# Expert layer: gate groups applied two steps later, gates read back in four parts, searches and row fetches spread differently

## The chip, the cores and the metric

The kernel runs on one core of one Trainium2 chip. The metric is the time of one execution on the device in microseconds (us). Before the change three executions took 3490.39, 3495.34 and 3495.37 us, median 3495.34. The profiled execution is a fourth one.

## The reference, cut to what matters

The reference is a stack of two transformer blocks followed by a third block (512 tokens, width 1024, all fp32). The change touches only the end of it, a layer of retrieved experts:

```
def peer_layer(h, w_q, sub_keys, u_tab, v_tab):          # T = 512 tokens, 8 heads, 128 x 128 experts
    q = (hf @ w_q).reshape(T, 8, 2, 128)
    s = einsum('thpd,hpnd->thpn', q, sub_keys)           # 128 scores for each half key
    sc, idx = top_k(s, 16)                               # for each half
    cand = sc[:, :, 0, :, None] + sc[:, :, 1, None, :]   # 256 sums
    top_sc, pos = top_k(cand, 16)                        # 16 experts per head, 128 per token
    eidx = take_along_axis(cidx, pos)
    gate = softmax(top_sc)
    act = gelu(einsum('thkd,td->thk', u_tab[eidx], hf))
    y   = einsum('thk,thkd->td', gate * act, v_tab[eidx])
```

Before that stand, in this order: two blocks with gated delta-net or stick-breaking attention, memory attention and an MLP, and one block with HGRN2, convolution and output projection.

## The kernel before, in words

The first 2130 us or so (all layers up to the experts) are not touched. The expert layer treats its four blocks of 128 tokens in two ways.

*By rows* (blocks 0 and 1). For each token, its 128 chosen expert rows are fetched from the table `peer_uv` (down and up vector side by side, 8 KB for each of 128 tokens). There are NROW = 256 such rows. Each row r costs one indirect DMA on GpSimd (L1287, waiting for `row_added` of the row that held its place before), one dot product on VectorE (`dot_row`, L3572), two tiny operations on ScalarE (`weigh_row`, L2699 and L2701: gelu and gate), and one multiply-add on VectorE (`add_row`, L3584). Ten places hold rows in flight; five of them, and in the gate stage only these, are outside the weight array.

*Densely* (blocks 2 and 3, 256 tokens). All 16384 experts are computed in 128 pairs of items. An "up" item (`up_unit`, L2025) multiplies 128 experts' down vectors with all 256 tokens, ScalarE takes the gelu into `weights` (L2668); a "down" item (`down_unit`, L2040) adds those weights times the up vectors into four banks that stay open. Each item loads 512 KB through the SP queue (L1088) into one of RAWS = 4 buffers; the load of item n waits for the end of item n - 4. Between the up and down items each weight has to be multiplied by the token's gate, which is zero for unchosen experts. The gates of 8 tokens (one group, NGATE = 32 groups) are made by 8 matmuls of one-hot matrices (`gate_products`, L2053): VectorE writes the one-hots (`one_hots`, L3534 and L3537), GpSimd two of them (`second_ones`, L1301), ScalarE scales six of them by the gate (`scale_ones`, L2689). The first half of the gates is applied at once on VectorE (`gate_weights`, L3548); ScalarE copies the second half out of the banks (`keep_gates`, L2677) and stores it in DRAM (`gate_half`, L2681). Two pairs of banks (4/5 and 6/7) alternate between groups.

The order of all engines follows one list, `STEPS`: 64 up items (the first stage; up to step 34 the query projection runs beside them), 32 gate groups (the gate stage), 128 alternating down and up items (the mixed stage, from `MIX_AT`), 4 "back" steps, then 64 down items (the last stage). Each engine walks the list in its own loop. The 256 rows are spread over it by `row_step`: 64 in the first stage, 10 in the gate stage, 120 in the mixed stage, 2 in the back steps, 60 in the last stage. The searches for the top 16 (`search`, a generator cut into pieces, eight for two heads) are handed out by `search_steps`: those of blocks 0, 2 and 3 in the first stage, those of block 1 (four groups, 32 pieces) one piece in each of 32 steps from `MIX_AT + 2` on.

The second half of the gates comes back from DRAM by `load_gates` on the SP queue (L1099), between item loads, and is applied by `later_weights` (L3560): in BACKS = 2 parts of 32 groups each, 128 KB a load, into LOADS = 8 buffers. Part 0 is applied one group a step from `MIX_AT + 67` on; part 1 in the four back steps, when all up items are done. The first down item of the second half (L2037) waits until every part is applied.

The names in the listing: `rows_at[s]` are the rows of step s, `gathers_at[s]` the fetches issued there, `full(engine, t)` waits until a bank is written, `have` until it is read out.

## Time and profile before

| | us |
|---|---|
| median of three executions | 3495.34 |
| profiled execution, its own time | 3504.54 |
| its span | 3502.8 |
| first stage and gate stage, from 2133 to 2718 | 585 |
| mixed stage, from 2718 to 3222 | 504 |
| back steps, from 3222 to 3247 | 25 |
| last stage and end, from 3247 | 256 |

The profiled execution took 9.2 us longer than the median. Over its whole span TensorE was busy for 92%, VectorE for 63%, ScalarE for 28%, GpSimd for 51%. In the two slices of the page that hold the gate stage the granted clock of TensorE is 6 tenths, elsewhere 9 or more. The bounds of the stages are read from the first and last matmuls of each line; busy times of a window are given as time and, in brackets, number of instructions.

### The profile page before, as it was taken

The numbers are of one execution on the slowest core, as the hardware profiler recorded it, in microseconds if no ns is written. First come the engines' busy times: TensorE is split into PE (matmuls) and PEld (weight loads), VectorE is DVE, ScalarE is ACT, GpSimd is POOL, SyncE is SP. The second block draws the span as 40 slices with busy tenths as digits, with TensorE's granted clock in tenths as the row PEclk, the third lists the DMA queues.
The fourth block names the chain that finished last, engine by engine and source line by source line (L and its number), as shares of the span: only waits on it lengthen the run. The fifth ranks groups of instructions, "written<-read, shape, count | busy, mean of one in ns | idle before, by whom it ended". The sixth has DMA issues, their size and how long they took to land.

```text
span 3502.8 us, 38167 instructions
## 1 busy us (share of the span) xinstructions
PE 3229.5 (92%) x13780; PEld 2400.8 (69%) x13780; DVE 2197.4 (63%) x3621; ACT 964.7 (28%) x2176; POOL 1797.9 (51%) x1008
## 2 busy tenths in 40 slices
PE   8999899999999999999999999997855989887998
PEld 5769778886767888688776677866755655554433
DVE  5764453337674333579465875889855996666765
ACT  4564431112174111211133423222344221111111
POOL 3544269997203999788865571222343343333420
PEclk9999999999999999999999999999966999999999
DMA  4430022232301322223322126767823899999996
GB/s 163 166 132 1 25 85 96 96 108 96 132 37 50 107 96 96 96 87 136 118 80 95 37 100 227 301 243 274 293 104 117 341 364 417 405 406 369 395 417 272
DMA packets 122368, 628.66 MB, mean 179 GB/s; under 512 B 13400, under 2 KB 21720, under 8 KB 66648
## 3 DMA queue, kind: packets, MB, share of 16 engines
q1 hardware_dynamic: 77104, 343.07, 26.6%
q0 software_dynamic: 36864, 268.45, 19.6%
q10 hardware_dynamic: 8232, 14.95, 1.1%
q8 instruction: 99, 1.62, 0.2%
q14 instruction: 69, 0.57, 0.1%
HBM read 607.55 MB, written 18.87 MB: 179 GB/s over the span
## 4 chain that ended last, share of the span: by engine, by line
PE 66%; DVE 15%; DMA 10%; ACT 4%; issue 4%; POOL 2%; DVEq 0%; ACTq 0%; POOLq 0%; SPq 0%
PE bank L1455 13%; PE bank L1456 13%; PE bank L1457 13%; PE bank L2040 6%; PE bank L2025 5%; DMA residual<-in_peer_vd 5%; DMA residual<-in_peer_ut 3%; DVE arena L3572 2%; ACT branch L2689 1%; DVE weight_ring L3584 1%; DVE squares L3403 1%; PE bank L1901 1%; PE bank L1883 1%; PE bank L1769 1%; PE bank L1402 1%
## 5 line engine op out<-in xcount | busy, mean ns | idle before, releaser
L1457 PE MATMUL bank<-split_arena 128*128 128x512 f32 x1776 | 696.8, 392 | 0.0
L1287 POOL DMA_INDIRECT arena<-in_peer_uv,rstd x181 | 266.4, 1472 | 633.0 <-DVE weight_ring L3584 345.7
L1194 POOL TENSOR_TENSOR split_arena<-weight_ring,ones 128x1024 fp32r<-128x1024 f32 x204 | 505.8, 2480 | 153.2 <-PE bank L1457 101.0
L1455 PE MATMUL bank<-split_arena 128*128 128x512 f32 x1392 | 546.7, 393 | 5.2 <-DVE split_normed L2930 2.5
L1456 PE MATMUL bank<-split_arena 128*128 128x512 f32 x1392 | 542.0, 389 | 0.0
L2025 PE MATMUL bank<-normed,residual 128*128 128x256 f32 x2048 | 481.4, 391 | 50.9 <-ACT arena L2668 38.6
L1196 POOL TENSOR_TENSOR split_arena<-weight_ring,split_arena 128x1024 fp32r<-128x1024 f32 x204 | 518.5, 2542 | 16.0
L2040 PE MATMUL bank<-residual,arena 128*128 128x512 f32 x1024 | 475.5, 611 | 45.4 <-DVE arena L3560 24.6
L2025 PEld LDWEIGHTS bank<-normed,residual 128*128 128x128 f32 x2048 | 396.6, 196 | 153.8 <-issue 65.6
L2040 PEld LDWEIGHTS bank<-residual,arena 128*128 128x128 f32 x1024 | 193.8, 194 | 288.4 <-issue 226.6
L1457 PEld LDWEIGHTS bank<-split_arena 128*128 128x128 f32 x1776 | 334.7, 188 | 73.5
L1163 POOL TENSOR_TENSOR split_arena<-weight_ring,split_arena 128x1024 fp32r<-128x1024 f32 x54 | 129.4, 2405 | 402.6 <-ACT split_arena L2179 350.7
L1455 PEld LDWEIGHTS bank<-split_arena 128*128 128x128 f32 x1392 | 261.6, 188 | 67.9 <-issue 8.6
L1456 PEld LDWEIGHTS bank<-split_arena 128*128 128x128 f32 x1392 | 261.6, 188 | 54.6 <-issue 1.5
L2699 ACT ACTIVATE row_gelu<-dots 128x1 f32<-128x1 f32 x256 | 51.6, 202 | 690.1 <-DVE dots L3572 689.9
L3572 DVE CUSTOM_DVE_ANT_0 arena<-arena,branch 128x1024 f32<-128x1024 f32 x181 | 220.3, 1221 | 34.0 <-DMA arena<-in_peer_uv,rstd 33.8
L1455 PE MATMUL bank<-split_normed,split_arena 128*128 128x512 f32 x560 | 223.7, 399 | 4.8 <-DVE split_arena L3207 3.8
L1456 PE MATMUL bank<-split_normed,split_arena 128*128 128x512 f32 x560 | 222.6, 397 | 0.0
L1287 POOL DMA_INDIRECT weight_ring<-in_peer_uv,rstd x75 | 106.0, 1414 | 190.1 <-DVE branch L3584 102.5
L2220 ACT ACTIVATE squares<-squares 128x512 f32<-128x512 f32 x64 | 40.4, 632 | 486.6 <-DVE squares L2845 486.6
L3220 DVE SCALAR_TENSOR_TENSOR bank<-arena,vector_columns,bank 128x512 f32<-128x512 f32 x232 | 153.3, 753 | 0.1
L2845 DVE SCALAR_TENSOR_TENSOR squares<-bank,rstd 128x512 f32<-128x512 f32 x64 | 44.1, 692 | 170.4 <-PE bank L1457 154.2
(509 smaller groups left out, 5265.6 us busy)
## 6 DMA issues: line engine op xcount, KB each, us to landing
residual<-in_peer_ut SPq DMA_DIRECT2D x128, 512.0 KB, 7.2
residual<-in_peer_vd SPq DMA_DIRECT2D x128, 512.0 KB, 11.1
weight_ring<-in_w_up SPq DMA_DIRECT2D x32, 1024.0 KB, 4.8
weight_ring<-in_w_down SPq DMA_DIRECT2D x32, 1024.0 KB, 4.7
weight_ring<-in_w_in SPq DMA_DIRECT2D x32, 1024.0 KB, 4.8
weight_ring<-in_ada_w SPq DMA_DIRECT2D x24, 1024.0 KB, 4.8
weight_ring<-in_w_in_a SPq DMA_DIRECT2D x12, 1024.0 KB, 6.7
weight_ring<-in_w_out SPq DMA_DIRECT2D x12, 1024.0 KB, 6.9
```

What stands on the lines that cost most here:

```text
L1163: pool.tensor_tensor(lo, raw(u)[:, :, h * P:(h + 1) * P], f32(hi), ALU.subtract).then_inc(split_ready, 1)
L1194: pool.tensor_tensor(hi, part, bc_mid(ones[:], DT), ALU.mult).then_inc(split_hi, 1)
L1196: pool.tensor_tensor(lo, part, f32(hi), ALU.subtract).then_inc(split_ready, 1)
L1287: pool.indirect_dma_start(row_places[i][0], None, a["peer_uv"], bass.IndirectOffsetOnAxis(ap=experts[n][:, c:c + 1], axis=0)).then_inc(row ...
L1455: pe.matmul(psum[t.bank][:], hi, a_hi[k], start=first, stop=False)
L1456: pe.matmul(psum[t.bank][:], lo, a_hi[k], start=False, stop=False)
L1457: return pe.matmul(psum[t.bank][:], hi, a_lo[k], start=False, stop=last)
L2025: m = pe.matmul(psum[t.bank][:, 0:DENSE], blk(raws[n % RAWS], k), H[:, k, DENSE:], start=k == 0, stop=k == DT - 1)
L2040: x = pe.matmul(psum[2 * b + c][:], blk(weights[:, m % WHALF, :], b), raws[n % RAWS][:, 512 * c:512 * (c + 1)], start=m == 0, stop=m == NK ...
L2699: act.activation(w, dots[:, r % RING8:r % RING8 + 1], ACT.Gelu).then_inc(row_gelu, 1)
L3220: m = dve.scalar_tensor_tensor(acc[i] if j < CONV_B - 1 else Y[:, k + i, :], glu[:, k + i, j:j + SEQ], vcol("conv_w_2", j * DT + k + i), a ...
L3572: dve.tensor_tensor_reduce(row, row, h_tok[:, n, :], 1.0, 0.0, ALU.mult, ALU.add, dots[:, r % RING8:r % RING8 + 1]).then_inc(row_dot, 1)
```

## The change

Four edits.

- In a gate step q, VectorE now writes the one-hots of group q and then applies the gates of group q - 2 (before: q - 1). ScalarE copies out group q - 2 ahead of scaling the one-hots of group q (before: group q - 1 behind it). Groups 30 and 31 are both finished in the first mixed step. The banks and buffers are the same.
- The 32 search pieces of block 1 stand in every fourth mixed step over 128 steps instead of in every one of the first 32.
- The second half of the gates comes back in BACKS = 4 parts of 16 experts' columns: 128 loads of 64 KB instead of 64 of 128 KB, into LOADS = 16 buffers of half the size (the same memory). Parts 0, 1 and 2 are applied in the mixed stage, two groups a step for 16 steps each, part 3 in the back steps, of which there are now two. The loads are placed by `back_load`: the first 16 of a part in pairs from 4 items ahead of the part's end, the other 16 in pairs 12 items behind it; for part 3 the latter all at item 195.
- 50 rows in the first stage instead of 64, and 24 in the gate stage instead of 10.

```diff
-LOADS = 8
-BACKS = 2
+LOADS = 16
+BACKS = 4
@@ in the plan
-        BACK_ITEM = WHALF + WHALF + 4
-        back_at = {MIX_AT + WHALF + 3 + q: q for q in range(NGATE)}
+        back_at = {MIX_AT + 2 * BACK_J * (p + 1) + 3 + i: (p, 2 * i) for p in range(BACKS - 1) for i in range(NGATE // 2)}
+        back_load = {}
+        for p in range(BACKS):
+            base = WHALF + 2 * BACK_J * (p + 1)
+            for i in range(NGATE):
+                n = base - 4 + i // 2 if i < LOADS else base + 12 + (i - LOADS) // 2
+                back_load.setdefault(min(n, 3 * WHALF + RAWS - 1), []).append(NGATE * p + i)
...
-        search_steps += range(MIX_AT + 2, MIX_AT + 2 + 64)
+        search_steps += range(MIX_AT + 2, MIX_AT + 2 + 32 * 4, 4)
...
-        gate_back = [k[:, i * UNIT_N:(i + 1) * UNIT_N] for k in keys_t for i in range(4)]
+        gate_back = [blk(k, i) for k in keys_t for i in range(8)]
...
-        for a0, a1, rows in ((3, G_AT, 64), (G_AT, MIX_AT, 10), (MIX_AT, BACK_AT, 120), (BACK_AT, LAST_AT, 2), (LAST_AT, LAST_AT + 58, 60)):
+        for a0, a1, rows in ((3, G_AT, 50), (G_AT, MIX_AT, 24), (MIX_AT, BACK_AT, 120), (BACK_AT, LAST_AT, 2), (LAST_AT, LAST_AT + 58, 60)):
@@ SyncE
-                elif BACK_ITEM <= n < BACK_ITEM + NGATE + LOADS:
-                    load_gates(n - BACK_ITEM)
-                elif n == 3 * WHALF + RAWS - 1:
-                    for q in range(NGATE + LOADS, BACKS * NGATE):
-                        load_gates(q)
+                for i in back_load.get(n, ()):
+                    load_gates(i)
+                if n == 3 * WHALF + RAWS - 1:
                     sp.dma_start(H[:, :, :], x_dram).then_inc(x_back, 16)
@@ ScalarE
+                if s < MIX_AT + 1 and s >= 2 and STEPS[s - 2][0] == "gate":
+                    keep_gates(STEPS[s - 2][1])
+                if s == MIX_AT:
+                    keep_gates(NGATE - 1)
                 if kind == "gate":
                     scale_ones(v)
-                if s and STEPS[s - 1][0] == "gate":
-                    keep_gates(STEPS[s - 1][1])
@@ VectorE
                 if kind == "gate":
                     one_hots(v)
-                    if v:
-                        gate_weights(v - 1)
+                    if v >= 2:
+                        gate_weights(v - 2)
                 elif kind == "back":
                     for q in range(LOADS * v, LOADS * (v + 1)):
-                        later_weights(1, q)
+                        later_weights(BACKS - 1, q)
                 elif s == MIX_AT:
+                    gate_weights(NGATE - 2)
                     gate_weights(NGATE - 1)
...
                 if s in back_at:
-                    later_weights(0, back_at[s])
+                    p, q = back_at[s]
+                    later_weights(p, q)
+                    later_weights(p, q + 1)
```

The order of VectorE in the middle of the gate stage, before. `mem_keys` and `mem_values` are the two one-hot buffers (even and odd groups), banks 4 and 5 hold even groups, 6 and 7 odd ones; `ISA` is a row's dot product, `SCALAR_TENSOR_TENSOR` a row's multiply-add:

```order
L3534 TENSOR_TENSOR mem_keys<-arena,masks 128x1024
L3537 TENSOR_TENSOR branch<-arena,masks 128x768
L3548 TENSOR_TENSOR arena<-arena,bank6 128x64x4
L3548 TENSOR_TENSOR arena<-arena,bank7 128x64x4
L3572 ISA weight_ring,dots<-weight_ring,branch 128x1024
L3572 ISA dots 128x1
L3534 TENSOR_TENSOR mem_values<-arena,masks 128x1024
L3537 TENSOR_TENSOR branch<-arena,masks 128x768
L3548 TENSOR_TENSOR arena<-arena,bank4 128x64x4
L3548 TENSOR_TENSOR arena<-arena,bank5 128x64x4
L3584 SCALAR_TENSOR_TENSOR weight_ring<-weight_ring,row_gelu 128x1024
```

And the same place now (the lines of the changed file are 5 higher here):

```order
L3539 TENSOR_TENSOR mem_keys<-arena,masks 128x1024
L3542 TENSOR_TENSOR branch<-arena,masks 128x768
L3553 TENSOR_TENSOR arena<-arena,bank4 128x64x4
L3553 TENSOR_TENSOR arena<-arena,bank5 128x64x4
L3577 ISA weight_ring,dots<-weight_ring,branch 128x1024
L3577 ISA dots 128x1
L3539 TENSOR_TENSOR mem_values<-arena,masks 128x1024
L3542 TENSOR_TENSOR branch<-arena,masks 128x768
L3553 TENSOR_TENSOR arena<-arena,bank6 128x64x4
L3553 TENSOR_TENSOR arena<-arena,bank7 128x64x4
L3589 SCALAR_TENSOR_TENSOR weight_ring<-weight_ring,row_gelu 128x1024
L3577 ISA arena,dots<-arena,branch 128x1024
```

Behind the one-hots of an even group now stand the products of the even group before it, not those of the odd group just computed, and rows follow more often.

SyncE's queue around the back steps, before; the waits are on `item_done` (`expert_unit_done`) and on `gate_used`:

```order
L1088 DMA residual<-in_peer_vd 128x1024 [waits expert_unit_done] x4
L1099 DMA mem_keys<-gate_half 128x256 [waits gate_half_used] x4
L1099 DMA mem_values<-gate_half 128x256 [waits gate_half_used] x4
L1099 DMA mem_keys<-gate_half 128x256 [waits gate_half_used] x4
L1099 DMA mem_values<-gate_half 128x256 [waits gate_half_used] x4
L1099 DMA mem_keys<-gate_half 128x256 [waits gate_half_used] x4
L1099 DMA mem_values<-gate_half 128x256 [waits gate_half_used] x4
L1116 DMA normed<-residual_copy 128x4096
```

And now:

```order
L1093 DMA residual<-in_peer_vd 128x1024 [waits expert_unit_done]
L1104 DMA mem_values<-gate_half 128x128 [waits gate_half_used] x2
L1093 DMA residual<-in_peer_vd 128x1024 [waits expert_unit_done]
L1104 DMA mem_values<-gate_half 128x128 [waits gate_half_used] x2
L1093 DMA residual<-in_peer_vd 128x1024 [waits expert_unit_done]
L1104 DMA mem_values<-gate_half 128x128 [waits gate_half_used] x2
L1104 DMA mem_keys<-gate_half 128x128 [waits gate_half_used] x8
L1104 DMA mem_values<-gate_half 128x128 [waits gate_half_used] x8
L1119 DMA normed<-residual_copy 128x4096
```

Behind the last item load of the mixed stage stood 24 loads of 128 KB; now 18 of 64 KB, and 14 more of the last part stand in pairs ahead of it, between the item loads.

## Rows read from the trace of the kernel before

**Rows 1.** Windows: PE, PEld, DVE, ACT, POOL busy us; granted clock, DMA share, GB/s.
```profile
2133.00:2320.00 187.00, 181.04 (x856) 144.51 (x855) 155.48 (x449) 54.12 (x134) 46.88 (x35) 0.99 0.76 282
2320.00:2523.00 203.00, 174.29 (x756) 142.23 (x754) 187.06 (x549) 57.81 (x150) 52.62 (x36) 0.94 0.78 283
2523.00:2718.00 195.00, 105.80 (x512) 98.66 (x512) 111.75 (x159) 81.97 (x277) 82.58 (x76) 0.67 0.31 111
2718.00:2850.00 132.00, 125.62 (x415) 81.16 (x416) 124.56 (x334) 27.86 (x85) 47.59 (x29) 0.96 0.93 358
2850.00:2990.00 140.00, 130.79 (x428) 81.31 (x427) 95.78 (x131) 26.11 (x91) 48.94 (x36) 0.98 1.00 402
2990.00:3222.00 232.00, 212.55 (x697) 133.53 (x695) 143.13 (x195) 36.24 (x139) 89.33 (x56) 0.96 1.00 402
3222.00:3247.00 25.00, 0.42 (x2) 0.42 (x2) 15.20 (x38) 1.38 (x5) 2.23 (x1) 0.60 0.84 300
```

**Rows 2.** Waits in the gate stage, 2523 to 2720: us, times, longest.
```profile
DVE arena L3548 <- ACT weight_ring L2677: 82.9, 32, 5.6
```

**Rows 3.** Timeline of two gate groups: start, duration, engine, operation, idle before.
```profile
2577.34 1.22 DVE L3534 TENSOR_TENSOR mem_values<-arena,masks 128x1024 f32<-128x1024 f32 x1
2579.47 1.86 ACT L2689 ACTIVATE branch<-branch,masks 128x128 f32<-128x128 f32 x6 [2.82 <-DVE branch L3537]
2581.54 3.75 PE L2053 MATMUL bank<-branch,mem_values 128*128 128x128 f32 x16 [1.47 <-issue]
2581.89 0.75 DVE L3548 TENSOR_TENSOR arena<-arena,bank 128x256 f32<-128x256 f32 x2 [2.46 <-ACT weight_ring L2677]
2582.56 1.22 DVE L3572 CUSTOM_DVE_ANT_0 arena<-arena,branch 128x1024 f32<-128x1024 f32 x1
2583.71 1.22 DVE L3534 TENSOR_TENSOR mem_keys<-arena,masks 128x1024 f32<-128x1024 f32 x1
2588.93 1.28 DVE L3584 SCALAR_TENSOR_TENSOR weight_ring<-arena,row_gelu,weight_ring 128x1024 f32<-128x1024 f32 x1
2590.13 1.22 DVE L3534 TENSOR_TENSOR mem_values<-arena,masks 128x1024 f32<-128x1024 f32 x1
```

**Rows 4.** GpSimd's one-hots (ns min/median/max; timeline, same columns) and a fetch.
```profile
L1301 POOL TENSOR_SCALAR branch<-arena,masks x64: 780/791/3661, 2523.4 to 2706.3; 128x128 f32<-128x128 f32 x64
...
2565.67 3.41 POOL L1301 TENSOR_SCALAR branch<-arena,masks 128x128 f32<-128x128 f32 x2 [2.10 <-PE bank L2053]
2572.48 1.75 POOL L1287 DMA_INDIRECT arena<-in_peer_uv,rstd  x1 [3.41 <-DVE weight_ring L3584]
```

**Rows 5.** Waits at the end of the first stage, 2330 to 2523.
```profile
PE bank L2025 <- ACT arena L2668: 25.8, 11, 4.4
```

**Rows 6.** VectorE's row adds, 2720 to 2850, grouped by line: busy us, mean ns.
```profile
L3584 DVE SCALAR_TENSOR_TENSOR weight_ring<-arena,row_gelu,weight_ring 128x1024 f32<-128x1024 f32 x19 | 24.4, 1283 | 4.0 <-ACT row_gelu L2701 3.5
L3584 DVE SCALAR_TENSOR_TENSOR weight_ring<-weight_ring,row_gelu 128x1024 f32<-128x1024 f32 x10 | 12.8, 1281 | 1.8 <-ACT row_gelu L2701 1.7
```

**Rows 7.** DMA queue 1 (packets, MB, share) and gate loads in two windows, 3250 to 3440 and 2990 to 3210.
```profile
q1 hardware_dynamic: 6935, 25.25, 33.5%
...
q1 hardware_dynamic: 13112, 33.45, 39.4%
...
mem_values<-gate_half SPq DMA_DIRECT2D x19, 128.0 KB, 12.0
mem_keys<-gate_half SPq DMA_DIRECT2D x16, 128.0 KB, 11.3
```

**Rows 8.** Waits for the gate loads in the mixed stage, 2980 to 3230.
```profile
DVE arena L3560 <- DMA mem_keys<-gate_half: 27.1, 9, 7.1
```

**Rows 9.** Timeline of the back steps.
```profile
3223.05 1.98 SPq L1099 DMA_DIRECT2D mem_keys<-gate_half  x4
3231.38 1.43 DVE L3560 TENSOR_TENSOR arena<-arena,mem_keys 128x256 f32<-128x256 f32 x4 [4.86 <-DMA mem_keys<-gate_half]
3246.61 9.75 PE L2040 MATMUL bank<-residual,arena 128*128 128x512 f32 x17 [24.58 <-DVE arena L3560]
```

More of the change, by code:

```diff
@@ L620, in build, with blk @@
         v_tiles = [item_tile(2 * NKEY - 1, b) for b in range(4)]
+        def blk(ap, n):
+            return ap[:, n * P:(n + 1) * P]
         q_f = region(0, LH)
@@ L977, in f32 @@
             return ap.bitcast(F32)
-        def blk(ap, n):
-            return ap[:, n * P:(n + 1) * P]
         def raw(u):
```

## The prediction

> **What bounds the kernel now.** I read the windows by stage first [rows 1], since the page's shares average over stages with different limits. Five limits follow one another there.
>
> From 2133 to 2320 TensorE is busy 181.0 of 187 us. From 2320 to 2523 it is busy 174.3 of 203, VectorE 187.1: there VectorE sets the pace, for up items wait for a bank that ScalarE empties late (25.8 us, [rows 5]), and ScalarE works in order behind the weighing of rows, which waits for VectorE's dot products. In the gate stage (195 us) nothing is full: TensorE 105.8, VectorE 111.8, ScalarE 82.0, DMA share 0.31, clock 0.67. That is a chain. In the first mixed window both TensorE (125.6 of 132) and VectorE (124.6) are nearly full and the DMA share is 0.93; from 2850 to 3222 the DMA share is 1.00 at 402 GB/s. In the back steps TensorE stands for 24.6 us behind `later_weights` [rows 9].
>
> The chain of the gate stage is seen in two groups of the timeline [rows 3]. VectorE starts one-hots at 2577.34, ScalarE scales from 2579.47 for 1.86 us and only then copies out the group before, VectorE multiplies that from 2581.89, after an idle 2.46 us, and at 2582.56 it is free again: 5.22 us a group, of which VectorE works 2.08 + 0.67. The waits add up to 82.9 us in 32 groups [rows 2]. A row adds its two big operations: the dot product 1.15 (2582.56 to 2583.71) and the add 1.20 (2588.93 to 2590.13), together 2.35. 32 x 5.22 + 10 x 2.35 = 190.5 us, and with the first group's start that is the 195 measured.
>
> **Gate stage, -41.** Now ScalarE copies group q - 2 ahead of the scaling, when its matmuls are long done, so the 82.9 us of waits go. What is late next? Two loops. VectorE's own work is 2.08 + 0.67 a group and 2.35 for each of 24 rows: 32 x 2.75 + 24 x 2.35 = 144.4 us, 4.5 a group. The other loop goes over two groups, since banks and one-hot buffers alternate: one-hots 2.08, scaling 1.86, matmuls 3.75 at 1.2 GHz [rows 3], and some 0.3 for four hand-overs: 8.0 for two groups, 4.0 a group or 128 us. VectorE's is the longer one. Two groups with two rows take VectorE 10.2 us, two with one row 7.85, so the second loop shows only in the latter, and hardly. With 6 us to start (the first matmuls come 6 us behind the window's beginning, since one-hots, scaling and one-hots on GpSimd stand in line) and 4 to finish groups 30 and 31 in one step, I take 154 us instead of 195: -41. The bounds: with VectorE busy all the time, -48 (147: the 111.8 busy us of [rows 1] plus 14 rows of 1.22 + 1.28 [rows 3]); with a step that stays at 5.22 for groups and hides the rows only in part, -15 (a rival, below). If TensorE's clock went to 2.4 GHz here the matmuls would halve, but VectorE would still pace. The waits added (none is new: the same semaphores one group earlier) hold nobody: behind VectorE's wait stand rows, and it has none to make.
>
> **First stage, -14.** 14 rows fewer are 14 x 2.35 = 33 us less for VectorE. By the planner's weights (32 steps of 6.1, 29 of 3.6) 9 of them leave the part beside the query projection, where TensorE is at 181.0 of 187: that gives 1 or 2 us at most. Five, and one or two of the 9 that fall behind 2320, leave the part that VectorE paces: 6.5 x 2.35 = 15 us. There VectorE would need 172, TensorE 174.3 of 203 before; two engines that are nearly equal don't overlap fully, so I take 190 for this window, -13, and -1 for the other. Bounds: -8 (half of it is waiting of another sort) and -28 (all of TensorE's idle time there).
>
> **Mixed stage, -6 and +10.** The block-1 searches: in the 130 us from 2720 VectorE adds 19 + 10 rows [rows 6], 29 x 2.35 = 68 us, of 124.6 busy, so searches are about 55. Three quarters of it, 41 us, move behind 2850, where VectorE is busy 239 of 372 us [rows 1]: it fits, VectorE goes to about 75%. In the first window TensorE then needs no waits, but the bytes are there too: 358 GB/s for 132 us is what 402 GB/s moves in 118. Between 0 and -14 I take -6, nearer to the middle, since TensorE was busy 125.6 already.
>
> The gate reload: the same 8.4 MB in twice as many packets. The price of a packet from [rows 7]: in the last stage queue 1 takes 33.5% of 16 x 190 us for 25.25 MB of 4 KB packets, 40.3 us of engine time per MB, 165 ns a packet. From 2990 to 3210 it takes 39.4% of 16 x 220 = 1387 us for 33.45 MB; 19 + 16 = 35 gate loads of 128 packets of 1 KB are 4.59 MB, the other 28.86 MB cost 1163 at 40.3, so 4480 small packets cost 224 us, 50 ns each. A straight line through 1 KB: 50 and 4 KB: 165 gives 31 ns for 512 B. Before, the mixed stage had 40 loads: 5120 x 50 / 16 = 16 us of all 16 engines. Now it has 110 (three parts of 32 and 14 of the last): 14080 x 31 / 16 = 27. The DMA share is 1.00 there, so the 11 us count nearly in full: +10. Bounds: +4 (a packet costs by its bytes alone, 25 ns) and +28 (50 ns whatever its size). That VectorE multiplies 96 halves with more instructions costs it some 5 us, hidden in its idle time, and 64 more issues cost SyncE 64 x 0.5 us [rows 9], hidden too: it waits for items nearly all the time.
>
> The Trainium skill says in "DMA: Bandwidth & Descriptors", section Bandwidth, that transfers under 64 KB are descriptor-dominated and gives 0.95 us for one of 64 KB against 6.15 for 1 MB. By that, 110 loads would hold the engines for 104 us, not 27, and the change would lose more than it gains. The trace speaks against it: 35 loads of 128 KB between 2990 and 3210 went through while the share stayed at 1.00 and the rate at 402 GB/s, because transfers of both queues run side by side. It strengthens the slower rival.
>
> **Back steps, -9.** Now 24 loads stand behind the last item, in rounds of 8 buffers, and the landings are 8.3 us (3223.05 to 3231.38) for the first, so three rounds make 24.6 us [rows 9]. Afterwards 14 of 32 loads have landed; 18 remain, at 0.5 us an issue (1.98 for four) 9 us, then one landing of 3 to 8 us and a last multiplication: 9 + 5 + 1.5 = 15.5. That is -9; bounds -16 (issue alone decides) and -3 (8.3 for a landing, and a second round for buffers 14 and 15).
>
> **Sum.** -41 - 14 - 6 + 10 - 9 = -60. Against the profiled execution's own 3504.5 that is 3444.5; this execution was 9.2 us above the median of 3495.3, so I expect the median at 3435.3, say 3435.
>
> **The rivals.**
> *A. GpSimd paces the gate stage.* Its two one-hots wait for the matmuls of q - 2 and stand behind fetches, which wait for a row add. With more rows they run against VectorE's big operations more often. For it: the pair took 3.41 us once, and single ones between 780 and 3661 ns [rows 4]. Then two groups take a fetch or two of 1.75, 3.41 and 3.75 of matmuls: up to 10.7, 5.3 a group, 171 us with start and end 180: only -15 in the stage, total -34, 3461. Against: the median is 791, and a fetch is issued right behind the add, a step before the one-hots can start. "GPSIMD Engine Reference" of the Trainium skill, Key points, has it that GpSimd shares its SBUF interfaces with VectorE and contends with VectorE operations that read two SBUF inputs; the spread in [rows 4] agrees, the median doesn't.
> *B. The reload eats more.* 50 ns for 512 B: +28 instead of +10, total -42, 3453.
> *C. All slack is given back.* First stage -28, first mixed window -14, back -16, gate -48, reload +4: -102, 3393; with half of the excess 3414.
> *D. The gate stage doesn't change.* If the wait had another cause than the copy (the clock, or GpSimd), the chain stays at 5.22 and 14 more rows cost 33 us there, while the first stage gives 14: with the other terms 0 to +14, about no change, 3495 to 3510.
> *E. Slower: the reload stalls VectorE.* The second 16 loads of a part are issued three steps ahead of their use, as before, and now there are two a step in 24 more steps. A wait was 3.0 us in the mean (27.1 in 9) and 7.1 at most [rows 8]. VectorE has 372 - 239 = 133 us idle in the DMA-bound windows; searches and extra instructions take 46 of them, 87 remain. Over 48 steps with reloads (three parts, 16 steps each), it saturates from 1.8 us a step, and each us more costs 48; beyond 3.1 the change loses its 60. At 4 us a step in all 48: 48 x 4 - 87 = +105, less 60: 3540. Against: half of the loads now have 11 steps' notice, so 24 steps at 3.0 are 72, which still fits.
>
> **How the numbers follow.** Chances: forecast 0.58 (its own range 3417 to 3452), A 0.14, B 0.09, C 0.11, D 0.04, E 0.04. From A at 3461 with some margin to the middle of C: 3404 to 3468. Within 0.2% (7 us, about what this kernel's measurement can tell) of 3495 lies most of D: 0.03. Slower: E and the rest of D, 0.04. Faster: 0.93.
>
> **What would show it.** In the gate stage, VectorE's wait for the copy near 0, its busy share over 90%, the window near 154 us; 170 or more with TensorE waiting for GpSimd's one-hots is A. The window from the first up item to the gate stage 14 us shorter. In the mixed stage the time from first to last item about 4 us longer than 504, with share 1.00, and packets of 512 B at 31 ns (50 is B); VectorE's waits for loads under 80 us (else E). TensorE's idle time in the back steps near 15. The forecast is wrong above all if VectorE isn't what ends last in the gate stage.

## The result, and the profile after

The changed kernel takes 3445.35 us (median of four, 3436.92 to 3446.74) against 3492.86 before (3488.27 to 3495.37): a ratio of 0.986, interval 0.984 to 0.9881. The forecast was 3435, range 3404 to 3468. The profiled execution's span fell from 3502.8 to 3444.1, by 58.7 us, where the sum said 60. The terms did much worse than the sum: two errors of 19 and 16 us, of opposite sign, nearly cancelled. The stages are read from the first and last matmuls of three lines: L2028 up items, L2056 gate groups, L2043 down items. For the changed kernel (instructions and their ns min/median/max, first and last start):

```profile
L2028 PE MATMUL bank<-normed,residual x2048: 379/379/796, 2150.1 to 3168.9; 128*128 128x256 f32 x187
L2056 PE MATMUL bank<-branch,mem_keys x256: 274/418/553, 2501.2 to 2660.8; 128*128 128x128 f32 x128
L2043 PE MATMUL bank<-residual,arena x1024: 592/592/1219, 2667.8 to 3430.2; 128*128 128x512 f32 x171
```

So the first stage is 2150.1 to 2501.2, the gate stage 2501.2 to 2667.7, the mixed stage up to 3168.9. The same lines of before give 2148.6, 2529.3, 2718.2 and 3221.7. Side by side, in us:

| | before | changed | difference | forecast |
|---|---|---|---|---|
| first stage | 380.7 | 351.1 | -29.6 | -14 |
| gate stage | 188.9 | 166.5 | -22.4 | -41 |
| mixed stage | 503.5 | 501.2 | -2.3 | +4 |
| TensorE idle in the back steps | 24.6 | 15.4 | -9.2 | -9 |
| last stage and end | 256.5 | 259.8 | +3.3 | 0 |

(1.5 us more lie ahead of the first item.) The windows of the changed kernel, with the columns of [rows 1]:

```profile
2135.00:2320.00 185.00, 182.49 (x867) 146.14 (x866) 150.00 (x471) 54.52 (x129) 42.92 (x30) 0.99 0.72 264
2320.00:2495.00 175.00, 166.21 (x750) 138.83 (x748) 158.90 (x488) 53.87 (x127) 34.97 (x26) 0.96 0.76 271
2495.00:2668.00 173.00, 97.31 (x513) 91.17 (x514) 144.42 (x201) 89.97 (x305) 163.28 (x90) 0.72 0.57 194
2668.00:2800.00 132.00, 123.76 (x405) 78.32 (x405) 91.66 (x162) 23.52 (x83) 51.75 (x31) 0.96 0.99 397
2800.00:2940.00 140.00, 126.56 (x418) 81.83 (x418) 103.77 (x207) 24.54 (x87) 53.29 (x33) 0.96 0.99 392
2940.00:3169.00 229.00, 210.54 (x715) 137.72 (x713) 174.40 (x350) 40.33 (x144) 90.12 (x56) 0.98 1.01 401
```

Against [rows 1]: in the gate stage (third line) GpSimd, 82.6 of 195 us before, is now busy 163.3 of 173, while VectorE, which was to pace it, has 28 us to spare. In the first mixed window VectorE fell from 124.6 to 91.7 us, and the DMA share rose from 0.93 to 0.99. Who waited in the gate stage:

```profile
PE bank L2056 <- POOL branch L1304: 64.5, 18, 6.9
ACT weight_ring L2680 <- PE bank L2056: 21.1, 12, 4.0
DVE arena L3553 <- ACT weight_ring L2680: 4.5, 2, 3.9
```

The wait of [rows 2], 82.9 us in 32, is down to 4.5 in 2. TensorE waits 64.5 us for GpSimd's one-hots (L1304). That wait alone proves little, for it was there before too. These two rows are of the kernel before, 2523 to 2720:

```profile
PE bank L2053 <- POOL branch L1301: 73.9, 22, 6.9
POOL branch L1301 <- PE bank L2053: 70.0, 20, 4.4
```

Then GpSimd in its turn waited 70.0 us for TensorE, and its one-hots were 3% of the chain that ended last. Now it waits 1.8 us for TensorE. The price of its one-hots is in the row by line (busy us, mean ns of one):

```profile
L1304 POOL TENSOR_SCALAR branch<-arena,masks 128x128 f32<-128x128 f32 x64 | 118.7, 1864 | 13.7 <-ACT masks L2155 10.9 <-PE bank L2056 1.8
```

and the chain that ended last through this stretch, by line, is clear:

```profile
by line: POOL branch L1304 67.9%; POOL arena L1290 13.7%; POOL weight_ring L1290 10.4%; PE bank L2056 4.5%; issue 3.9%; ACT weight_ring L2680 0.4%; PE bank L2043 0.4%; DVE arena L3553 0.3%; DVEq L3588 0.0%; POOLq L1283 0.0%; ACTq L935 0.0%
```

Before, the same 64 instructions took 63.0 us, 991 ns each; 92% of the chain is now GpSimd's one-hots and fetches. The timeline shows when they are slow:

```profile
2583.93 1.57 POOL L1304 TENSOR_SCALAR branch<-arena,masks 128x128 f32<-128x128 f32 x2
2585.60 1.22 DVE L3539 TENSOR_TENSOR mem_values<-arena,masks 128x1024 f32<-128x1024 f32 x1 [2.60 <-PE bank L2056]
...
2587.77 8.56 POOL L1304 TENSOR_SCALAR branch<-arena,masks 128x128 f32<-128x128 f32 x4
2588.27 1.28 DVE L3589 SCALAR_TENSOR_TENSOR weight_ring<-weight_ring,row_gelu 128x1024 f32<-128x1024 f32 x1
2589.47 1.22 DVE L3577 CUSTOM_DVE_ANT_0 arena<-arena,branch 128x1024 f32<-128x1024 f32 x1
2590.61 1.22 DVE L3539 TENSOR_TENSOR mem_keys<-arena,masks 128x1024 f32<-128x1024 f32 x1
2591.75 1.04 DVE L3542 TENSOR_TENSOR branch<-arena,masks 128x768 f32<-128x768 f32 x1
2592.44 3.75 PE L2056 MATMUL bank<-branch,mem_values 128*128 128x128 f32 x16 [3.96 <-POOL branch L1304]
```

Two one-hots take 1.57 us while VectorE stands idle (2583.93), and four take 8.56 beside its uninterrupted operations (from 2587.77), 2.1 each. TensorE starts on a group when that group's two are done, at 2592.44 for the first pair. Laid beside VectorE's operations in the two traces, 51 of the 64 one-hots before overlap none of them (by less than 0.05 us) and take 790 ns in the mean; in the changed kernel only 12 do, with 794 ns. An estimate from the same overlaps: the 64 one-hots are 50.6 us of work at 790 ns. In the changed kernel 5.0 us of their time lay beside no operation of VectorE, 21.7 beside `gate_weights` (one input in PSUM) and 92.6 beside operations whose large inputs both lie in SBUF. If they ran at full speed in the first two, the other 23.9 us of work took 92.6 us: about a quarter of the speed.

In the back steps the loads of part 3 follow one another now:

```profile
3171.10 1.71 DVE L3565 TENSOR_TENSOR arena<-arena,mem_keys 128x128 f32<-128x128 f32 x8 [5.85 <-ACT arena L2671]
3172.49 4.29 SPq L1104 DMA_DIRECT2D mem_keys<-gate_half  x8
3174.96 0.49 DVE L3565 TENSOR_TENSOR arena<-arena,mem_values 128x128 f32<-128x128 f32 x2 [2.16 <-DMA mem_values<-gate_half]
3176.83 4.03 SPq L1104 DMA_DIRECT2D mem_values<-gate_half  x8
3182.77 1.70 DVE L3565 TENSOR_TENSOR arena<-arena,mem_values 128x128 f32<-128x128 f32 x8
3184.61 2.04 PE L2043 MATMUL bank<-residual,arena 128*128 128x512 f32 x2 [15.36 <-DVE arena L3565]
```

With [rows 9] this is 15.36 us of idle TensorE against 24.58. The 16 last loads are issued at 0.5 us each, from 3172.49 to 3180.86, but VectorE waits for none of them. It waits, last at 3179.60, for the loads issued just ahead; the chain has one landing of 8.03 us there, from 3171.54:

```profile
3171.54 8.03 DMA mem_values<-gate_half
```

Behind it come VectorE's own 4.9 us: two groups, a row's dot product and the last 16 groups.

### The profile page after: what moved, and what is told of

It reads as the page before. It is cut to its first block, busy times and chain, and to the rows that moved or that the text cites. A ratio compares the mean times of both kernels' runs of the same rounds, so it can differ in the third digit from the quotient of the medians.

```text
span 3444.1 us, 38297 instructions
## 1 busy us (share of the span) xinstructions
PE 3208.0 (93%) x13780; PEld 2395.6 (70%) x13780; DVE 2201.9 (64%) x3685; ACT 968.3 (28%) x2176; POOL 1869.0 (54%) x1008
## 4 chain that ended last, share of the span: by engine, by line
PE 74%; DMA 9%; DVE 7%; POOL 6%; ACT 2%; issue 2%; SPq 0%; DVEq 0%; ACTq 0%; POOLq 0%
PE bank L1458 13%; PE bank L1459 13%; PE bank L1460 13%; PE bank L2028 10%; PE bank L2043 8%; DMA residual<-in_peer_vd 6%; POOL branch L1304 3%; DMA residual<-in_peer_ut 2%; PE bank L1975 2%; PE bank L1904 1%; PE bank L1886 1%; PE bank L1772 1%; PE bank L1405 1%; PE bank L1650 1%; PE bank L1660 1%
## 5 line engine op out<-in xcount | busy, mean ns | idle before, releaser
L2028 PE MATMUL bank<-normed,residual 128*128 128x256 f32 x2048 | 479.1, 390 | 42.6 <-DMA residual<-in_peer_ut 34.3
L2028 PEld LDWEIGHTS bank<-normed,residual 128*128 128x128 f32 x2048 | 398.4, 196 | 138.2 <-DMA residual<-in_peer_ut 48.3
L2043 PE MATMUL bank<-residual,arena 128*128 128x512 f32 x1024 | 467.1, 603 | 28.2 <-DVE arena L3565 15.4
L2043 PEld LDWEIGHTS bank<-residual,arena 128*128 128x128 f32 x1024 | 192.1, 192 | 263.2 <-issue 213.9
L3577 DVE CUSTOM_DVE_ANT_0 arena<-arena,branch 128x1024 f32<-128x1024 f32 x178 | 216.9, 1219 | 18.8 <-DMA arena<-in_peer_uv,rstd 18.7
L1290 POOL DMA_INDIRECT weight_ring<-in_peer_uv,rstd x78 | 120.9, 1550 | 184.4 <-DVE branch L3589 99.0
L3589 DVE SCALAR_TENSOR_TENSOR weight_ring<-arena,row_gelu,weight_ring 128x1024 f32<-128x1024 f32 x92 | 117.8, 1281 | 62.7 <-ACT row_gelu L2704 60.5
```

The costliest lines, as they stand in the source:

```text
L1290: pool.indirect_dma_start(row_places[i][0], None, a["peer_uv"], bass.IndirectOffsetOnAxis(ap=experts[n][:, c:c + 1], axis=0)).then_inc(row ...
L2028: m = pe.matmul(psum[t.bank][:, 0:DENSE], blk(raws[n % RAWS], k), H[:, k, DENSE:], start=k == 0, stop=k == DT - 1)
L2043: x = pe.matmul(psum[2 * b + c][:], blk(weights[:, m % WHALF, :], b), raws[n % RAWS][:, 512 * c:512 * (c + 1)], start=m == 0, stop=m == NK ...
L3577: dve.tensor_tensor_reduce(row, row, h_tok[:, n, :], 1.0, 0.0, ALU.mult, ALU.add, dots[:, r % RING8:r % RING8 + 1]).then_inc(row_dot, 1)
L3589: m = dve.scalar_tensor_tensor(row_acc[n], row, w, row_acc[n], ALU.mult, ALU.add)
```

## The experiments

My theory after the traces: the gate stage is paced by GpSimd (rival A of the prediction); every row taken from the first stage is worth most of its 2.35 us; of the two edits in the mixed stage one gains and the other loses it. Twelve runs. "Before" below is the kernel before in the same series (medians 3496.10, 3498.08 and 3497.19 in the three series). The changed kernel was timed only with the result, where before had 3492.86, so a difference from it in us compares two series whose level differs by 3 to 5 us. The profiled execution of before, 3504.54, lies 6 to 12 us above all these medians.

**a_two_behind.** The first edit alone.

```diff
@@ ScalarE: keep_gates of group q - 2, ahead of scale_ones(q); VectorE:
-                    if v:
-                        gate_weights(v - 1)
+                    if v >= 2:
+                        gate_weights(v - 2)
```

> The kernel before with only the first edit: gates applied and copied out two groups later, rows (64 and 10), searches and the two-part reload as before. From first matmul of the gate stage to the first down item it took 188.9 us before and 166.5 with all edits. Theory 1 (GpSimd's one-hots, slowed by VectorE, pace the gate stage once the copy is off the chain): with 14 fewer rows there are fewer fetches and fewer big VectorE operations beside them, so about 145 us, the one-hot pairs on GpSimd still above 2 us in the mean, and the total 40 to 45 us below before. Theory 2 (the loop of VectorE's one-hots, scaling and matmuls at 1.2 GHz paces): 4.0 us a group, 128 to 135 us, total 53 to 60 below. First stage unchanged at 381 (within 3) by both.

Measured: 3455.10 us, ratio 0.988 (0.9865 to 0.9894), -41 us. Gate stage 143.2 (theory 1 had said 145), first stage 378.8. GpSimd's one-hots took 1868 ns each in the mean. They are 58.6% of the chain through the stage, in which VectorE is busy only 75% of the time. So GpSimd is in the way even with 10 rows, and the edit alone gives most of the change's gain.

**b_rows.** The fourth edit alone.

```diff
-        for a0, a1, rows in ((3, G_AT, 64), (G_AT, MIX_AT, 10), ...
+        for a0, a1, rows in ((3, G_AT, 50), (G_AT, MIX_AT, 24), ...
```

> The kernel before with only the row edit: 50 rows in the first stage, 24 in the gate stage. First stage (first up item to first gate matmul, 380.7 before, 351.1 with all edits): by the prediction's term 14 us shorter, by the trace of the changed kernel 30 shorter, which I now expect, since no other edit touches that stage. Gate stage with the old order: each row adds its 2.35 us to a chain of 5.22, so 188.9 + 33 = 222. If instead rows fall into the 2.46 us waits, under 200. Total with the chain: about +3 (between -2 and +8); with rows in the waits: -20.

Measured: 3505.05, ratio 1.0019 (1.001 to 1.0028), +9. First stage 350.4, as in the changed kernel; gate stage 219.7. In the old chain a row costs 2.2 us (30.8 for 14), nearly its full 2.35, so alone the edit gives back in the gate stage what it wins in the first. Beside the first edit it pays a little: against a_two_behind the changed kernel's first stage is 27.7 us shorter and its gate stage 23.3 longer.

**c_search.** The second edit alone.

```diff
-        search_steps += range(MIX_AT + 2, MIX_AT + 2 + 64)
+        search_steps += range(MIX_AT + 2, MIX_AT + 2 + 32 * 4, 4)
```

> The kernel before with only the search edit: block 1's 32 search pieces in every fourth mixed step. The prediction took -6 for it. If the early mixed window was held by VectorE: mixed stage (first down item to last up item, 503.5 before) about 6 shorter, total -6 (to -12). If DMA bytes hold the whole mixed stage, what is won early is lost later: within 3 us of no change.

Measured: 3482.98, ratio 0.996 (0.9946 to 0.9974), -13. The mixed stage is 484.7, not 503.5: three times the forecast's term. (With the stage's code unchanged, a_two_behind and b_rows have 501.1 and 501.4, so 16 to 19 us are won there; the timed runs show 13 in all.) The whole mixed stage, before and in this run:

```profile
2718.00:3222.00 504.00, 468.96 (x1536) 296.01 (x1536) 363.47 (x657) 90.21 (x315) 185.86 (x120) 0.97 0.98 390
```

```profile
2713.00:3197.00 484.00, 459.86 (x1534) 290.24 (x1533) 361.09 (x653) 88.35 (x314) 196.95 (x120) 0.99 1.00 403
```

The same work at 403 instead of 390 GB/s, and TensorE's idle time 24 us instead of 35, its busy time 9 shorter at a mean clock of 0.99 instead of 0.97.

**d_back.** The third edit alone (BACKS = 4, LOADS = 16 and the placing of loads and products).

```diff
-LOADS = 8
-BACKS = 2
+LOADS = 16
+BACKS = 4
```

> The kernel before with only the reload in four parts. The prediction took +10 in the mixed stage for smaller packets and -9 in the back steps, together about 0. The trace of the changed kernel has 15.4 us of idle TensorE in the back steps instead of 24.6, and a mixed stage of 501.2 instead of 503.5 with searches spread as well. If small packets cost by bytes plus a few ns (27 ns seen): mixed stage +3 to +6, total -4 to -6. If the +10 is there and the search edit hid it: total 0.

Measured: 3507.47, ratio 1.0027 (1.0016 to 1.0037), +11: neither expectation. Mixed stage 514.8 (+11.3, where the prediction had +10), idle TensorE in the back steps 10.9 (-13.6), last stage and end 260.6 instead of 256.5. By its trace the edit comes out even, by its timed runs it loses; the trace of before is of an execution 8.4 us above this series' median, that of d_back 2 below its own, and this is most of the difference. Against the 501.1 and 501.4 of a_two_behind and b_rows the mixed stage is over 13 us longer. Like the row edit it is no gain alone; two_parts below asks whether it is one in company.

**hot1 and hot0.** Less of the one-hot work on GpSimd, from the changed kernel.

```diff
-POOL_HOT = 2
+POOL_HOT = 1
```

> The changed kernel with one second-side one-hot a group on GpSimd instead of two (VectorE and ScalarE take seven instead of six). VectorE gets 0.14 us a group more, ScalarE 0.31. If GpSimd paces the gate stage (its pair took 1.6 us alone and 4.3 to 5.5 beside VectorE's operations): gate stage 166.5 to about 152, total 12 to 15 below the changed kernel. If VectorE paces: gate stage about 4 us longer. If the matmuls at 1.2 GHz pace: unchanged.

```diff
-POOL_HOT = 2
+POOL_HOT = 0
@@ TensorE
-                pe.wait_ge(pool_hot, q + 1)
@@ GpSimd
-                    second_ones(v)
+                    pass
```

> The changed kernel with all eight second-side one-hots on VectorE and ScalarE, none on GpSimd (and TensorE doesn't wait for GpSimd in the gate stage). VectorE has 2.08 + 0.27 + 0.67 = 3.02 us a group and 24 x 2.35 for rows: 153 us, so a gate stage of about 157: 9 us below the changed kernel if GpSimd paces it now, and 9 us above it if VectorE does.

Measured: 3434.47 (ratio 0.9819, 0.98 to 0.9838) and 3436.85 (0.9821, 0.9804 to 0.9838). Gate stages 150.5 and 151.3 instead of 166.5, nearly the length of VectorE's own work. The window and the chain of hot1 in that stage:

```profile
2499.00:2650.00 151.00, 93.82 (x513) 87.10 (x514) 144.23 (x197) 95.20 (x328) 117.47 (x57) 0.73 0.69 229
```

```profile
by line: PE bank L2056 32.0%; issue 11.2%; DVE branch L3542 9.5%; ACT branch L2692 8.8%; DVE weight_ring L3589 8.8%; DVE mem_values L3539 7.3%; DVE mem_keys L3539 6.6%; DVE arena L3553 5.9%; DVE arena L3577 4.5%; DVE weight_ring L3577 3.8%;
```

No GpSimd line is left in the chain; VectorE is busy 144.2 of 151. The stage is close to what the prediction's sum for VectorE gave (144.4 plus ends), and the GpSimd term is 16 of the 19 us that were missing. In the total 8.5 to 11 us of them arrive by the medians, 14 by the ratios to before: the mixed stage was 513 and 514, 501 in the changed kernel (below).

**rows57 and rows43.** The row edit in other sizes, from the changed kernel.

```diff
-        for a0, a1, rows in ((3, G_AT, 50), (G_AT, MIX_AT, 24), ...
+        for a0, a1, rows in ((3, G_AT, 57), (G_AT, MIX_AT, 17), ...
```

> The changed kernel with 57 rows in the first stage and 17 in the gate stage. By the traces 14 rows gave 29.6 us in the first stage, 2.1 us a row: first stage 366. Gate stage: with GpSimd pacing, each row costs a fetch of 1.5 to 2 us and the contention of two big operations, so 7 fewer give about -14, 152; with VectorE pacing 7 x 2.35 = -16. Total within 3 us of the changed kernel.

```diff
-        for a0, a1, rows in ((3, G_AT, 50), (G_AT, MIX_AT, 24), ...
+        for a0, a1, rows in ((3, G_AT, 43), (G_AT, MIX_AT, 31), ...
```

> The changed kernel with 43 rows in the first stage and 31 in the gate stage. TensorE is busy 348.7 of the 360 us before the gate stage now, so the first stage can give only 5 to 8 us more, while the gate stage grows by 15 (7 x 2.1 to 2.35): total +8. If the first stage still gave 2.1 us a row: total 0.

Measured: 3447.73 (0.9859, 0.9839 to 0.9878) and 3457.53 (0.9888, 0.9869 to 0.9907). The stages by rows in the first stage, with b_rows and a_two_behind:

| rows first / gate | first stage | gate stage (two behind) |
|---|---|---|
| 64 / 10 | 380.7 (before) | 143.2 |
| 57 / 17 | 363.7 | 149.9 |
| 50 / 24 | 351.1 | 166.5 |
| 43 / 31 | 346.3 | 177.2 |

The first seven rows give 17.0 us by this table. But the four kernels with 64 rows there have 376.4 to 381.8 us, so it is 13 to 18, some 2.2 for each row, nearly all of its VectorE time. The next seven give 12.6; the last seven 4.8, when TensorE has become the limit (busy 332.5 of 347 us). 50 and 57 can't be told apart in total, 43 is worse.

**two_parts.** The change without its reload edit.

```diff
-LOADS = 16
-BACKS = 4
+LOADS = 8
+BACKS = 2
@@ and back_at, the placing of loads and the back steps as before
```

> The changed kernel without its reload edit: gates two groups behind, 50 and 24 rows, spread searches, but the second half's gates back in two parts of 128 KB loads. Alone, the search edit shortened the mixed stage by 18.8 us and the reload edit lengthened it by 11.3. If the reload in four parts costs the mixed stage more than it gives in the back steps (my theory now): mixed stage 485, back steps 25 of idle TensorE, total 8 to 12 below the changed kernel. If its gain in the back steps (9 to 13 us) outweighs it: total 0 to 5 above the changed kernel.

Measured: 3430.82 (3428.56 to 3434.00), ratio 0.9806 (0.9788 to 0.9824), below the changed kernel's whole interval. Mixed stage 487.0, idle TensorE in the back steps 25.4. The reload edit costs the change some 14 us. By the traces, from this kernel to the changed one: mixed stage +14.2 (501.2 less 487.0), back steps -10.0, last stage +2.2, and, what no term of the sum had, gate stage +7.7 (166.5 for 158.8). The last is no chance value: half_loads below, in two parts, has 158.9 again, even_parts, in four, 166.6. Why the gate stage is longer with four parts isn't shown.

**half_loads.** From two_parts.

```diff
-                sp.dma_start(gate_back[n % LOADS], weights_dram[q][:, part * BACK_J * GTOK:(part + 1) * BACK_J * GTOK]).then_inc(
-                    gate_landed[n % LOADS], 16)
+                for x in range(2):
+                    at = part * BACK_J * GTOK + x * P
+                    sp.dma_start(gate_back[n % LOADS][:, x * P:(x + 1) * P], weights_dram[q][:, at:at + P]).then_inc(
+                        gate_landed[n % LOADS], 16)
```

> As the run two_parts, but each 128 KB load of gates is issued as two of 64 KB (packets of 512 B, twice the issues), at the same places and with the same use. If size and number of the packets make the four-part reload slow: mixed stage 10 or more above that of two_parts (485), total +10. If packets cost 27 ns, the mixed stage gets 4 us longer, total +4 to +5, and the rest of the loss is in where the loads stand (bursts of two a step behind which item loads queue).

Measured: 3439.92 (3436.05 to 3442.78), ratio 0.9828 (0.9809 to 0.9846), +9 on two_parts with no overlap of the runs. Mixed stage 493.6, 6.6 longer, back steps 29.6, 4.2 longer. So halving the loads, with bytes and places unchanged, costs 9 us. The packets' own time explains about 5 of them (16384 packets at 30 ns for 8192 at 50, over 16 engines, by the prices below).

**even_parts.** From the changed kernel.

```diff
-                n = base - 4 + i // 2 if i < LOADS else base + 12 + (i - LOADS) // 2
+                n = base - 1 + 29 * i // 32 if p < BACKS - 1 else base - 8 + i
@@ back_at: group i of part p at MIX_AT + 2 * BACK_J * (p + 1) + 3 + 29 * i // 32
```

> The changed kernel (four parts), but with loads and products spread evenly: about one load an item and one group a step over 29 of 32 steps, instead of two a step in half of them. If the bursts cost the time (theory), the mixed stage falls from 501 to 516 in the runs with bursts to about 490, total 8 to 15 below the changed kernel. If the number of packets or the bytes cost it, no change (within 3 us).

Measured: 3439.06 (3434.87 to 3446.53), ratio 0.9831 (0.9811 to 0.9851), 6 below the changed kernel with overlapping intervals: suggestive, not proven. Mixed stage 499.3. In the trace VectorE waits 2.5 us for the gate loads where the changed kernel has 45.4, so the placing does take away waits; nearly all of the stage's length stays. Against two_parts, in the same series, four parts placed evenly are still 8 us slower.

**two_parts_hot1.** Both findings together: two_parts with `POOL_HOT = 1`.

```diff
-POOL_HOT = 2
+POOL_HOT = 1
```

> As the run two_parts, with one one-hot a group on GpSimd instead of two. If both gains add: gate stage 151 instead of 166, mixed stage 485, total 20 to 25 below the changed kernel, about 3422. If the faster gate stage only reaches a DMA-bound mixed stage earlier and is given back there (the run hot1 had 513 in the mixed stage, the changed kernel 501): total only 8 to 12 below.

Measured: 3417.73 (3407.64 to 3419.95), ratio 0.9769 (0.9751 to 0.9786): 79 us below before, 28 below the changed kernel, the best of all. Against hot1, which differs by the reload edit alone, it is 17 us faster: a second pair for what that edit costs. Gate stage 150.3, and the mixed stage 481.3 at 408 GB/s, by the trace of its fastest execution, 10 us below its median:

```profile
2643.00:3125.00 482.00, 460.81 (x1536) 290.81 (x1536) 361.67 (x654) 89.13 (x314) 195.87 (x120) 0.99 1.01 408
3125.00:3150.00 25.00, 0.09 (x1) 0.12 (x1) 15.27 (x41) 2.66 (x6) 0.94 (x1) 0.60 0.93 340
```

## Why the prediction was right, and where only by luck

*The total* was right: -58.7 in the profiled execution for -60. In the medians it is -47.5, because the profiled execution of before lay 11.7 us above its median (I had corrected by 9.2) and the one after at its median. The assumption that the two executions sit equally high cost 10 us. That the sum hit the trace within 1.3 us was luck: the gate stage gave 19 us less than forecast and the first stage 16 more, and neither error has to do with the other.

*Gate stage, -41: too much by 19.* Half of the mechanism held: the copy's wait went from 82.9 to 4.5 us, and VectorE's work is 144 us. What failed is the step "VectorE's is the longer one" of two loops. There is a third engine, GpSimd, and it was rival A: two one-hots stretched to 3.7 us in the mean beside VectorE, plus a fetch of about 1.7 for three groups in four, 5 us a group. Only A's loop was off: it had 3.75 us of matmuls in it, but the chain has 4.5% of matmuls, for the one-hots of two groups run back to back. I set it aside since "the median is 791". That median came from a stage in which VectorE stood idle 2.46 us in every group, and it was those idle times that the one-hots ran in. The edit filled them. By the Trainium skill, "GPSIMD Engine Reference", Key points, GpSimd shares its SBUF interfaces with VectorE and contends with VectorE instructions that have two SBUF inputs. The traces agree: 991 ns became 1864 in the mean, and the quarter of the speed was beside just such operations. hot1 shows the price, 16 us.

*First stage, -14: half of what came.* I took seven or eight of the 14 rows as nearly worthless because TensorE was busy 181 of 187 us in the first window. Up to 2320 that was so. But VectorE, as I read it, fell behind there and the debt was called in right after (from 2300 to 2460 TensorE stood idle for 28 us before, and for 8 from 2300 to 2430 in the changed kernel): the query projection's last matmul started 235.1 us after the first item before, and 221.9 in the changed kernel, so 13 of the 30 us came ahead of step 35. About 7 of the 30 aren't idle time at all: the same 1502 matmul records were busy for 343.3 us before and 336.1 now, with a granted clock of 0.88 from 2372 to 2460 before against 0.92 from 2350 to 2430 now. rows57 gives some 2.2 us for each of the first seven rows, nearly VectorE's full price.

*Searches, -6: mis-sized,* -18.8 in the mixed stage when alone. The step that failed is "TensorE was busy 125.6 already", which looked at the first window alone. Counted by the item loads issued, some 5 us are won in the first 125 us of the stage, as forecast, and another 10 in the next 124, where I took the share of 1.00 at 402 GB/s for a limit: from 2743 to 2985 c_search moves 408 to 417 GB/s. By these traces even my bound of -14 was too small.

*Reload, +10 and -9.* d_back has +11.3 and -13.6. The changed kernel's 15.4 us in the back steps hit the forecast's 15.5 by luck: the issues of the last loads, 9 us of that sum, held nobody, and five other kernels with four parts have 10.9 to 12.0 us (d_back, hot1, hot0, rows57, rows43), even_parts 12.8. The packet price was good: by queue 1 in the changed kernel, a window in the mixed stage and one in the last:

```profile
q1 hardware_dynamic: 15825, 33.08, 39.6%
...
mem_keys<-gate_half SPq DMA_DIRECT2D x32, 64.0 KB, 13.2
mem_values<-gate_half SPq DMA_DIRECT2D x26, 64.0 KB, 10.4
```

```profile
q1 hardware_dynamic: 6851, 24.98, 32.9%
```

The first is 220 us long, the second 190. The last stage gives 0.329 x 16 x 190 / 24.98 = 40.0 us per MB; 58 loads are 3.80 MB, the other 29.28 MB cost 1171 of 0.396 x 16 x 220 = 1394 us, and 223 us for 7424 packets are 30 ns; the forecast was 31. But next to spread searches the edit did more harm than the sum had: its mixed stage is 14.2 us longer than that of two_parts. Of these half_loads shows 6.6 for the halving; an estimate for another 5 is the 1.97 MB that four parts move from the back steps into this stage (55 times 128 KB for 40), at 402 GB/s. Landings didn't get shorter with size (13.2 and 10.4 us for 64 KB, [rows 7] had 11.3 and 12.0 for 128 KB). The Trainium skill's rule in "DMA: Bandwidth & Descriptors", section Bandwidth, that transfers under 64 KB are descriptor-dominated, pointed the right way for these of 64 KB, but its 0.95 us for one, from a table of transfers that GpSimd issues, is far too much here: the 110 loads of the mixed stage would make 104 us. And the last stage is 3.3 us longer. All seven kernels with shorter back steps have 258.3 to 260.6 us there, those with the old ones 256.1 to 257.6. I read it so that fetches run ahead while TensorE stands idle, since the stage is DMA-bound; no run separates this.

*The slower rival* E didn't come: VectorE's waits for the loads were 45 us, below 80.

What stays open: the mixed stage of the kernels with four parts and spread searches was 499 (even_parts), 501 (changed), 511, 513, 514 and 516 (rows57, hot1, hot0, rows43), more than the row or one-hot edits account for, and the gate stage is 8 us longer with four parts than with two, with the same operations. How the loads' places meet the fetches', and the one-hots VectorE's operations, may shift with small offsets; no run here settles it.

## What to carry to other kernels

When an edit removes an engine's waits, look at who worked undisturbed in them: the durations of a neighbour that are read from the old trace hold only for the old idle times. A window in which one engine is full says nothing of the debt that another builds up in it; count work that is removed up to the point where that debt is paid. And split a change before keeping it: one of these four edits lost 14 us of what the others won.

## What the runs showed of the hardware

GpSimd's 128x128 tensor_scalar took 790 ns in the mean where no operation of VectorE overlapped it, and ran at about a quarter of that speed beside operations of VectorE whose large inputs both lie in SBUF. That is an estimate from the overlaps; a fit over eleven of the traces gives 0.18 to 0.34 of the speed beside the three kinds of them (one-hots, dot products, row adds) and 1.0 beside `gate_weights`, which has one input in PSUM. Its mean was 991 ns before, 1864 in the changed kernel, 1868 in a_two_behind with VectorE less busy, and 2529 in hot1 (up to 3792), where one is left a group: what counts is what it runs beside, more than VectorE's share.

Halving 32 x 2 loads of 128 KB into 64 KB cost 9 us at full DMA load, though 512 B packets took 30 ns against 50 for 1 KB, which is 5 us. SyncE took 0.5 us to issue a load of either size. At a DMA share of 1.00 to 1.02 the rate was 402 GB/s before and up to 417 in c_search.

In the mixed stage the same matmuls were busy for 469.0 and 468.4 us where the granted clock of TensorE was 0.97 and 0.95 in the mean (before, d_back), and for 459.9 and 460.8 where it was 0.99 (c_search, two_parts_hot1). TensorE stood idle 35 and 46 us in the first two, 24 and 21 in the others, and cut into sixteen slices, the stages of c_search and d_back have a granted clock below 1.00 only in slices in which TensorE stood idle for 3 us or more. A stall costs more than its own length.
